# The second half of chunk 0 in another order: weight halves first, convolution taps and the transposes of z last

## The reference

```
h = rmsnorm(x, norm_g);  u = h @ w_in              # 1024 x 2816, eleven splits of 256
a_b, a_c, a_x, a_g, b_v, b_a, b_g, c_u, c_g, x_q, x_g = split(u)
y_a = a_b * conv3(a_c * a_x) * silu(a_g)
z   = layernorm(conv31(b_v * sigmoid(b_a)) + bias)
y_b = silu(z) * silu(b_g)
y_c = (pool_w @ (trailing_means(c_u) - c_u) + pool_bias) * pool_scale * silu(c_g)
y_x = softmax(q k / 8) v * silu(x_g)                # 4 heads, 256 memory tokens
out = rmsnorm(x + concat(y_a, y_b, y_c, y_x) @ w_out, final_norm_g)
```

## Time and profile before

| what | value |
|---|---|
| three runs | 1484.26, 1485.45, 1485.58 us, median 1485.45 |
| the profiled execution | 1489.08 us, its span 1487.3 us |
| TensorE busy | 1439.3 us, 97% of the span |
| VectorE busy | 1175.1 us, 79% |
| ScalarE busy | 563.8 us, 38% |
| GpSimd busy | 221.8 us, 15% |
| mean granted TensorE clock | 0.99 |

### The profile page before, as it was taken

How to read it: one execution, slowest core, us unless ns; L and a number is a source line. 1 busy time by engine, 2 the same in 40 slices (tenths; PEclk the granted TensorE clock), 3 DMA queues, 4 the chain that set the end, 5 groups by cost and what they waited for, 6 DMA issues and landing times.

```text
span 1487.3 us, 32647 instructions
## 1 busy us (share of the span) xinstructions
PE 1439.3 (97%) x11758; PEld 1230.1 (83%) x11758; DVE 1175.1 (79%) x3088; ACT 563.8 (38%) x1238; POOL 221.8 (15%) x180
## 2 busy tenths in 40 slices
PE   5979999999999999999999999999999999999996
PEld 4767888888888888888888888888888888888874
DVE  6996795969779595968869596977959597896865
ACT  6773342433333243423423243333324342332323
POOL 0162110111111011111110011111101111111110
PEclk9989999999999999999999999999999999999999
DMA  9986436455644635565563545564463556446374
GB/s 270 257 311 213 184 105 221 170 184 197 222 174 126 252 120 207 178 217 191 164 237 100 216 173 189 197 213 182 123 246 125 195 186 226 184 149 228 106 246 162
DMA packets 128386, 284.16 MB, mean 191 GB/s; under 512 B 12393, under 2 KB 69405, under 8 KB 128349
## 3 DMA queue, kind: packets, MB, share of 16 engines
q1 hardware_dynamic: 128349, 283.68, 55.4%
HBM read 225.60 MB, written 58.03 MB: 191 GB/s over the span
## 4 chain that ended last, share of the span: by engine, by line
PE 90%; DMA 3%; DVE 2%; ACT 1%; issue 1%; POOL 0%; SPq 0%; ACTq 0%; DVEq 0%
PE u L529 21%; PE u L530 21%; PE u L531 21%; PE sps L529 5%; PE sps L531 4%; PE sps L530 4%; PE qps L529 4%; PE qps L531 3%; PE qps L530 3%; DMA ring<-wo_split 3%; PE ops L610 2%; PE sps L741 1%; DMA rows<-in_w_out 1%; DVE z L1392 1%; PE u L666 0%
## 5 line engine op out<-in xcount | busy, mean ns | idle before, releaser
L529 PE MATMUL u<-h_hi,w_hl 128*128 128x256 f16 (+1 forms) x2992 | 791.1, 270 | 13.3 <-ACT gate L894 5.3
L530 PE MATMUL u<-h_lo,w_hl 128*128 128x256 f16 (+1 forms) x2992 | 790.3, 270 | 0.0
L531 PE MATMUL u<-h_hi,w_hl 128*128 128x256 f16 (+1 forms) x2992 | 790.0, 270 | 0.0
L1392 DVE SCALAR_TENSOR_TENSOR z<-glu,cst,z 128x256 f32<-128x256 f32 (+1 forms) x1020 | 425.5, 489 | 0.5
L529 PEld LDWEIGHTS u<-h_hi,w_hl 128*128 128x128 f16 x2992 | 293.8, 99 | 59.9 <-issue 8.1
L531 PEld LDWEIGHTS u<-h_hi,w_hl 128*128 128x128 f16 x2992 | 293.7, 99 | 33.7
L530 PEld LDWEIGHTS u<-h_lo,w_hl 128*128 128x128 f16 x2992 | 293.7, 99 | 33.2 <-issue 0.7
L894 ACT ACTIVATE gate<-u,inv 128x256 f32<-128x256 f32 (+1 forms) x204 | 82.8, 457 | 124.9 <-PE u L531 124.7
L1838 POOL TENSOR_TENSOR sa<-cu 128x540 f32<-128x540 f32 (+1 forms) x17 | 30.7, 1804 | 566.4 <-ACT cu L894 501.8
L529 PE MATMUL sps<-ring,y_hi 128*128 128x512 f32 (+1 forms) x262 | 104.7, 400 | 0.2 <-POOL y_lo L1824 0.2
L529 PE MATMUL qps<-ring,y_hi 128*128 128x512 f32 x258 | 102.8, 398 | 1.2 <-DMA ring<-wo_split 1.2
(11 more groups left out here) (226 smaller groups left out, 1854.3 us busy)
## 6 DMA issues: line engine op xcount, KB each, us to landing
ring<-wo_split SPq DMA_DIRECT2D x256, 512.0 KB, 7.9
ob<-in_x_prompt SPq DMA_DIRECT2D x34, 512.0 KB, 4.1
probs_turned<-probs SPq DMA_DIRECT2D x130, 128.0 KB, 2.4
pt<-probs_turned SPq DMA_DIRECT2D x32, 512.0 KB, 3.5
out<-ob SPq DMA_DIRECT2D x32, 512.0 KB, 3.4
rows_turned<-rows SPq DMA_DIRECT2D x114, 128.0 KB, 2.4
w_hl<-in_w_in SPq DMA_DIRECT2D x20, 512.0 KB, 7.3
wo_split<-ring SPq DMA_DIRECT2D x16, 512.0 KB, 4.8
```

What stands on the lines that cost most here:

```text
L529: nc.tensor.matmul(out, a_hi, b_hi, start=first, stop=False)
L530: nc.tensor.matmul(out, a_hi, b_lo, start=False, stop=False)
L531: return nc.tensor.matmul(out, a_lo, b_hi, start=False, stop=last)
L1392: ins = nc.vector.scalar_tensor_tensor(z[:, c, 0:n], glu[:, c, k:k + n], w, z[:, c, 0:n], ALU.mult, ALU.add)
```

## The change

Only chunk 0's lists change, and one buffer. No instruction is added or taken away.

- `FIRST`: the slot of w10 moves from behind b_g to right behind w9, and TensorE makes the sums of w10 there. `w_square(20)` and `w_square(21)` follow `w_square(19)`.
- ScalarE: the high weight halves 15 to 21 move forward, and the pieces 1 to 15 of W_out are spread further back; a_g's gate comes ahead of `d_high`.
- VectorE: `w_scale(9)`, `w_scale(10)` and the low weight halves come earlier, the taps from 21 on come last; `yx_out` comes ahead of `z_stats`.
- TensorE: `attend(0, N, 0)` moves behind x_g; the out pieces run in the order of `FIRST_PIECES` (both halves of y_a and the first half of y_c first); `attend(0, N, 1)` comes behind six of them, `z_rows` behind eight, `z_back` behind twelve; both `next_rows` come ahead of the last four.
- SP: `probs_leave(0)` comes behind `load_piece(12)` and no longer behind `load_piece(15)`; `keep(9)` and `load_piece(13)` stand between it and `probs_arrive(0)`; the rest follows. The ring's loads wait for the pieces in their new order.
- The four raw buffers of W_out lie in y_lo's memory (`raw_w`) instead of `rows`; POOL waits for all 16 low halves before the first `y_low`.

```diff
-         "w9", "a_b", "a_g", "b_g", "w10", "c_g", "mix", "x_g", "zf", "zb", "r0", "r1", "r2", "r3"]
+         "w9", "w10", "a_b", "a_g", "b_g", "c_g", "mix", "x_g", "zf", "zb", "r0", "r1", "r2", "r3"]
...
+FIRST_PIECES = [0, 1, 2, 3, 6, 7, 4, 5, *range(8, PIECES)]
...
         y_hi = sb("y_hi", [P, KT, N], F32R)
+        with nc.sbuf_tensor("raw_w", [P, RAW * HALF], F32) as raw_w:
+            raws = [raw_w[:, b * HALF:(b + 1) * HALF] for b in range(RAW)]
         y_lo = sb("y_lo", [P, KT, N], F32R)
...
-            for p in range(RAW, PIECES):
+            for p in range(RAW, 13):
                 keep(p - RAW)
                 load_piece(p)
...
-                sp.wait_ge(o_piece.sem, o_piece.at(i, q - RING + 1))
+                done = q - RING + 1
+                if type(i) is int and i == 0:
+                    done = FIRST_PIECES.index(q - RING) + 1
+                sp.wait_ge(o_piece.sem, o_piece.at(i, done))
...
                 probs_leave(0, 0, N)
+                keep(13 - RAW)
+                load_piece(13)
+                probs_arrive(0, 0, N)
+                for p in range(14, PIECES):
+                    keep(p - RAW)
+                    load_piece(p)
                 for p in range(PIECES - RAW, PIECES):
                     keep(p)
-                probs_arrive(0, 0, N)
                 probs_across(0, 1, N)
...
-                for q in range(q0, q1):
+                for q in FIRST_PIECES[q0:q1] if type(i) is int and i == 0 else range(q0, q1):
...
                 weight_sums(9)
+                weight_sums(10)
                 project(0, N, "a_b")
                 project(0, N, "a_g")
                 scores(0, N, 1)
                 project(0, N, "b_g")
-                weight_sums(10)
                 project(0, N, "c_g")
-                attend(0, N, 0)
                 mix(0, N)
                 project(0, N, "x_g")
+                attend(0, N, 0)
+                out_begin(0, N)
+                out_pieces(0, N, 0, 6)
+                attend(0, N, 1)
+                out_pieces(0, N, 6, 8)
                 z_rows(0, N)
-                attend(0, N, 1)
-                out_begin(0, N)
-                out_pieces(0, N, 0, Z_AT)
+                out_pieces(0, N, 8, PIECES - 2 * CT)
                 z_back(0, N)
-                out_pieces(0, N, Z_AT, PIECES - 2 * CT)
                 next_rows(0, xb)
+                next_rows(1, xp)
                 out_pieces(0, N, PIECES - 2 * CT, PIECES)
-                next_rows(1, xp)
...
                 w_square(19)
-                piece_hi(1)
+                act.wait_ge(wsq_ok.sem, 20)
+                w_square(20)
+                w_square(21)
                 scaled_out(0, N, "a_c", gate[:, 1, :, 0:N], ACT.Copy, ac_ok)
                 w_high(15)
...
                 w_low(15)
-                taps(0, N, 21, 22)
+                w_scale(9)
+                w_scale(10)
+                w_low(16)
+                w_low(17)
+                conv_a_taps(0, N)
                 pool_diff(0, N)
-                w_low(16)
-                w_scale(9)
+                ab_out(0, N)
                 softmax_rcp(0, N, 0)
-                conv_a_taps(0, N)
-                taps(0, N, 22, 23)
-                w_low(17)
-                ab_out(0, N)
+                for k in range(18, 20):
+                    w_low(k)
                 probs_lo(0, N, 0)
+                d_low(0, N)
                 softmax_max(0, N, 1)
-                w_low(18)
-                taps(0, N, 23, 24)
-                w_low(19)
-                taps(0, N, 24, 25)
-                ya_out(0, N)
-                d_low(0, N)
-                w_scale(10)
-                softmax_rcp(0, N, 1)
                 for k in range(20, 22):
                     w_low(k)
+                ya_out(0, N)
+                taps(0, N, 21, 23)
+                softmax_rcp(0, N, 1)
                 probs_lo(0, N, 1)
-                taps(0, N, 25, 31)
+                taps(0, N, 23, 31)
+                yx_out(0, N)
                 z_stats(0, N)
-                yx_out(0, N)
...
                 for k in range(0, 16):
                     piece_lo(k)
+                pool.wait_ge(wo_lo_ok.sem, PIECES)
                 y_low(0, N, 0, ya[:, :, 0:N], 0)
```

More of the change, by code:

```diff
@@ L134, in encoder_program @@
             turned = [rows[:, t * D:(t + 1) * D] for t in range(2)]
-            raws = [rows[:, b * HALF:(b + 1) * HALF] for b in range(RAW)]
             st_rows = rows[:, D:D + 3 * GW]
@@ L1147, in first_chunk @@
                 w_square(19)
[L1148 removed]
+                act.wait_ge(wsq_ok.sem, 20)
+                w_square(20)
+                w_square(21)
                 scaled_out(0, N, "a_c", gate[:, 1, :, 0:N], ACT.Copy, ac_ok)
                 w_high(15)
[L1151 to L1152 removed]
+                piece_hi(1)
                 w_high(16)
[L1154 to L1165 removed]
+                piece_hi(2)
+                w_high(17)
+                piece_hi(3)
+                exps(0, N, 0)
+                w_high(18)
+                piece_hi(4)
+                w_high(19)
+                piece_hi(5)
+                act.wait_ge(wsq_ok.sem, FT)
+                scaled_out(0, N, "a_g", gate[:, 2, :, 0:N], ACT.Silu, ag_ok)
                 d_high(0, N)
                 probs_hi(0, N, 0)
[L1168 to L1170 removed]
+                piece_hi(6)
+                w_high(20)
+                w_high(21)
+                for k in range(7, 9):
                     piece_hi(k)
[L1172 to L1174 removed]
+                b_gate(0, N)
                 exps(0, N, 1)
[L1176 to L1177 removed]
+                for k in range(9, 11):
+                    piece_hi(k)
                 probs_hi(0, N, 1)
[L1179 removed]
+                y_high(0, N, 0, ya[:, :, 0:N], ya_ok)
+                for k in range(11, 13):
+                    piece_hi(k)
+                c_gate(0, N)
                 mixed(0, N)
[L1181 to L1182 removed]
+                for k in range(13, 16):
+                    piece_hi(k)
                 scaled_out(0, N, "x_g", gate[:, 2, :, 0:N], ACT.Silu, xg_ok)
```

24 lines of the change are left out of this document (removed).

## The result

| comparison | changed kernel, us | kernel before beside it, us | ratio, 95% interval |
|---|---|---|---|
| first | 1504.91 (1501.09 to 1506.42, 4 runs) | 1485.51 (4 runs) | 1.0125 [1.011, 1.0141] |
| second | 1501.96 (1500.72 to 1504.86, 4 runs) | 1486.37 (8 runs) | 1.0102 [1.0079, 1.0126] |
| third | 1502.24 (1502.12 to 1504.85, 5 runs) | 1486.77 (17 runs) | 1.0112 [1.0093, 1.0131] |

The change costs 15 to 19 us, 1.0% to 1.25%. The forecast was +12 us, 1497, and at most 1502.5: the direction is right, the size is short by 3 to 7 us, and the first comparison lies above the range. The profiled execution is the quickest of its four, 1501.09 us.

A forecast was written before the change was run, and what follows sets the result against it. Chunk 1's first projection start was taken to bound the kernel: 129.4 (first out piece) + 34.7 (behind it) + 5.5 (clock) = 169.6 against 157.4, +12.2 us, median 1497; range 1488.5 to 1502.5.

The forecast's parts named there:

- Front, "gains 14.5 us": Chunk 0 up to x_g: earlier weight scales and halves end x_g at 113.5 instead of 128.0, 14.5 us gained.
- T: Moment the first out piece of chunk 0 can run: forecast 129.4, bounds 124 to 132; before, 129.31.
- The chain: SP, ScalarE and POOL waits from probs_leave(0) through second exponentials, piece_hi(9) and take-back to last pieces; gives back all 14.5 us.
- The table load: ScalarE's second exponentials: 3.2 us with load by the profile row, chosen over the skill page's 4.6, which gives 130.8.
- Behind T: First out piece to chunk 1: 34.7 us against 26.4 before, from new stalls behind attend(1) and at the next rows.
- Clock 5.5: TensorE's granted clock falls behind three stalls of over 2 us: 5.5 us lost together, bounds 3 and 8.
- The sum in the profile: Chunk 1's start: 129.4 + 34.7 + 5.5 = 169.6 against 157.4, +12.2 us.
- the effective 157.4: Kernel before's chunk 1 start, 155.74, counting the 1.7 us clock loss behind it.
- terms are differences inside that span and are added to the median: Method: differences inside the 1487.3 us profiled span are added to the median, the profiled execution being 3.6 us above it.
- the shorter chain (+3 to +8): Rival: few POOL and VectorE clashes, fast landings, clock 3; 1488.5 to 1493.5 us; chance 0.24.
- faster: Rival: first out piece stands ready when TensorE comes, about 1482; decides at 119.7 with small clock loss; chance 0.07.
- no difference: Rival: within 0.2% (3 us), first out piece near 117 to 123 with small clock loss; chance 0.07.

The follow-up runs named there:

- The runs that open the chain: On the changed kernel: take-back of pair 0 right behind its stores, pieces ahead of the second exponentials, or both with further reordering; ratios 1.0011 to 1.0094.
- The tail alone: On the kernel before: old front kept, only the changed order of out pieces, attend(1), z_rows and next_rows behind x_g; 1497.12 us, ratio 1.0068.
- the new tail: On the changed kernel: z_rows behind four out pieces, other work behind attend(1), pieces between the two next_rows, yx_out behind z_stats; 1495.11 us, ratio 1.0072.
- the runs that only open the front: On the changed kernel, order behind the first out piece untouched: earlier take-back, pieces ahead of the second exponentials, or both with more moves; ratios 1.0093, 1.0094, 1.0073.
- the kernel before's second trace: The kernel before profiled again without an edit; profiled execution 1491.99 us, against a median of 1489.80 over 17 runs.

## Why the prediction was right or wrong, step by step

- **Front, "gains 14.5 us"**: 17.0 measured; x_g ended 2.5 us before the forecast, since VectorE had the last low weight halves done at 106.6 for 109.4. It changed nothing, as the text had it, since T doesn't hang on x_g.
- **The chain**: its shape is right at each link, its terms off by up to 2.7 us and of both signs. probs_leave(0) 105.17 for 107.9; the stores took 5.6 us to release the exponentials for 4.4; these began at 110.79 for 112.3; take-back 116.77 for 118.1; attend(0) 122.66 for 123.3; load_piece(15) 119.69 for 121.4, but 6.6 us to its reader for 4.6. T 130.07 for 129.4. That T agrees to 0.7 is in part luck, since terms of both signs cancel. The runs that open the chain show that it is one (T 122.8 to 127.7), and that it has two strands, which the prediction didn't say: it had ScalarE's strand only as a sum in passing.
- **The table load**: the row was the right choice. Load, four exponentials and their reads took 3.2 us (110.79 to 114.02), as in the earlier trace rows, and the first exponential started 1.30 us after the load did. A load right behind other work shows no more: ScalarE's piece ends at 118.31, the load starts at 118.32, the next instruction at 119.62. The drain of 1.38 us that the Trainium skill, ScalarE: Activation LUTs, What ACT_TABLE_LOAD costs, adds is in none of these places.
- **Behind T**: 34.7 us forecast without the clock; measured 37.7 less 5.3, so 32.4. The stall behind attend(1) is 2.91 for 2.9; those at the next rows are 3.5 together (1.71, 0.70, 1.11) for 5.3; the 0.4 before piece 2 did not come, since pieces 0 and 1 ran at the low clock over it. The differences that the prediction lists beside it add up to 7.8 and not to 8.3. The tail alone, put on the kernel before, cost 10 us, and the new tail gave 6.5 us back at chunk 1, so the stalls are causes and no bystanders.
- **Clock 5.5**: 5.3 in the profile, 5.0 and 6.6 in the two others, and up to 7.6 in the runs that only open the front.
- **The sum in the profile**: the spans differ by 12.0 us for 12.2 forecast. That is closer than its parts, and in part luck. Chunk 1 stood at 167.75 for 169.6, which makes 10.4 over the effective 157.4; the other 1.6 us lie in later chunks. TensorE waits there 2.6 us for the ring and waited 1.2, but the kernel before's second trace has 3.1 and the changed kernel's two others 3.6 and 2.5, so this can't be put on the change. And the kernel before's first trace has a fall of the clock near its end that neither its second nor the changed kernel's first or third has, and that costs 1.5 us (4.52 x 0.34):

```profile
1421.00:1426.00 5.00, 4.52 (x15) 3.73 (x16) 1.90 (x6) 1.21 (x2) 0.00 (x0) 0.66 0.47 170
```

- **The step that failed** is "terms are differences inside that span and are added to the median". As a difference of two profiled executions the sum held (12.0); as a difference of medians it did not: 19.4, 15.6 and 15.5. The profiled execution of before lay 3.6 us above its median, the second one 2.2 above its own: the stretches measured against were those of executions longer than usual. The changed kernel's three lay 3.8 below, 2.9 above and at their medians. The means of the profiled executions, 1502.7 and 1490.5, differ by 12.2 us. With the positions, 2.9 + 0.3 = 3.2 us, this makes 15.4, the difference of the second and third comparison. This is arithmetic and no cause. Of the 3.6 the fall near 1421 explains some 1.5; what else the quicker executions of before have less of, no trace shows, since none of them was profiled, and it stays open.
- **A term that was missing**: clock that comes and goes. The first comparison lies another 4 us above the two others. Its three executions that were not profiled had a mean granted clock of 0.984 to 0.985, the profiled one 0.989; the second trace (0.984) shows where such a difference can lie: at 80 to 87 us and near 1440, with T 1.3 us later and the remainder behind chunk 1's start 2.7 us longer than in the first. The third (0.987) has neither fall. This puts 2 to 4 us between executions of one kernel; that it explains the 4 us of the first comparison is argued and not shown. 1501.96 and 1502.24 of the later comparisons lie just under the forecast's upper end.

Of the rivals, the shorter chain (+3 to +8), "faster" and "no difference" are refuted by the time, and the last two by T as well. The point of decision given for "faster", T = 119.7 with the old tail's stalls, stays untried: the earliest T reached was 122.80. Nor was the new front run with the old tail, which would price the chain alone. Whether the place of the raw pieces is worth anything wasn't tried alone: in `rows` they share memory with the take-back's target, which the new order writes while pieces are still read.

## What to carry to other kernels

The length of a wait in a profile is not its price: ask what sets the next instruction behind it. Here 9 us less in front of attend(0) moved the end by 0.6, while four stalls of 0.7 to 2.9 us in the tail, each with work at hand that could have stood in it, were worth 6.5, clock included.

When instructions are put ahead of a wait on one engine, write down for every in-order list what stands behind each wait and who waits for that; two lists that wait on each other in turn (stores, exponentials, pieces, keeps, take-back) close into a chain that no busy share shows. And set a forecast of half a per cent against the median only after the profiled execution's own distance to it is allowed for.

## What the runs showed that was not expected

- The same stall does not always bring the clock down: 1.8 us of wait at 80 us is followed by clock 1.00 in the changed kernel's first and third trace and by 0.51 until 87 in its second. A wait of 2.0 us near the end, the same in all five traces of the two kernels, is followed by 0.66 over 5 us in one trace of the kernel before and by 1.00 in the other.
- Under a full load of transfers (DMA share 1.01, 410 GB/s from 122 to 130 us in the changed kernel) a raw piece took 6.6 us from issue to its reader. The row of four `keep` at 120.74 (8.02 us) is no sign of the load: its four issues take 0.3 to 0.6 us each, at 120.74, 123.26, 126.64 and 128.44, and SP waits between them for POOL's low halves.
- POOL against VectorE, in the changed kernel too: the 16 instructions of eight taps next to POOL's last pieces took 11.49 us, 0.72 each, for 0.40 each in the earlier trace rows. Which of the two pays differs between executions: the same 12 instructions of before took 4.80 us while POOL's low half of y_a took 2.94, and in its second trace 6.82 us while that low half took 1.35 and another product on POOL 1.44.
